# Centring the values and initial states in the projection stage, and a chunk norm whose variance comes spread over channels

## The chip, the cores and the metric

The kernel runs on one core of one Trainium2 chip. The metric is the device time of one execution in microseconds (us). A core has TensorE (PE: matmuls, with its weight loads shown apart as PEld), VectorE (DVE), ScalarE (ACT), GpSimd (POOL) and SyncE (SP), which here only issues transfers. Each engine works through its own list of instructions in order; they wait for each other by semaphores.

## What is computed

One layer of a bidirectional mixer over 1,024 latent tokens and 128 context tokens, D_MODEL 1,024, 16 heads of 64 channels, with an MLP behind it. What matters here, from the reference:

```python
S = S * w_t[:, :, None, :] + sa[..., None] * b_t[:, :, None, :] + v_t[..., None] * k_t[:, :, None, :]
...
wkv = ys[0] + ys[1]
mu = jnp.mean(wkv, axis=-1, keepdims=True)
var = jnp.mean(jnp.square(wkv - mu), axis=-1, keepdims=True)
ln = ((wkv - mu) * lax.rsqrt(var + LNX_EPS)).reshape(B, T, D_RWKV) * p['lnx_w'] + p['lnx_b']
x_a = (ln + (bonuses[0] + bonuses[1]).reshape(B, T, D_RWKV)).astype(xn.dtype) * g_out
```

The scan output `y` of a token is linear in the values `v` and in the initial state along the value channel. If each value vector and each state column has its mean over the 64 value channels taken off beforehand, `y` comes out with mean zero over its head. The bonus still needs the values as they are. Context tokens start from a zero state, and their final states are outputs that need the uncentred values.

## The kernel before

Channels lie on the 128 partitions, two heads (a *pair*) at a time, so there are 8 pairs. Tokens are cut into 9 chunks of 128: 8 of latents, 1 of context. The order of each engine's work is written out by hand in five blocks of the program (sync, gpsimd, tensor, scalar, vector), and all waits are explicit. There are three stages.

**Projection stage** (function bodies of the loops `for p in range(PAIRS)` on each engine). For each pair PE fills PSUM banks in a fixed list, `Fills` (L104): 12 low-rank fills, then for k, r, v, ks, cc, ch, vt, cb, g, za, bon, zb three fills each (thirds of the tokens, `cg`), g having six. Fill n goes to bank (n + 6) mod 8 and waits until fill n - 8 has been emptied (`freed`, L129), so the fill `g1` of the last third waits for the emptying of `cb` of the first third, and `g0` of the last third for `vt` of the last third. `BY_DVE` (L101) names the fills that DVE empties, in that order; ACT empties the others. `vt` is the transposed values; ACT copies it to `vn` (L1616), SP stores it to HBM (L674), and `vn` also serves as room for the small inversions (`substitution`, L2013). DVE's own list in a pair: running sums of log decays, keys, the substitution of the last pair, the key norm (reciprocal over 1,152 columns, L2057), operands, the product `ch` (L2071), the convolution (L2076 to L2083), the product `cb` (L2088), the bonus (L2093).

**Scan stage**: 72 units, u = 9 p + j (pair p, chunk j; j = 8 is the context chunk). In loop step s PE runs turn, token_major, ur_state, the first Gram products of unit s + 4, serial_ur, `spread`, left, y_state, the second Gram products, serial_u, right, `mean`, serial_s, serial_y, `gate` and `variance` (L1348 to L1388). DVE in step s runs `reciprocal`, the addition of half the outputs (`y_add`, L2161: for j = 4 to 7 of the step before), `turned`, `carried`, Gram mask 0, `scaled`, `summed`, `centred`, the new states, Gram mask 1 (L2202 to L2233). The masks (`gram`, L2106) copy the one Gram PSUM tile out; PE may fill it again only then. In steps 9 to 23 DVE also does pieces of the last pair's substitution before and after.

The norm of a finished chunk (`finals`, L177) goes: PE sums y over channels (`mean`), DVE subtracts (`centred`), ACT squares, PE sums the squares per head into 2 columns (`variance`, one row per token), ACT takes the root of 128x2 (`deviation`), DVE the reciprocal of 128x2, PE spreads it back over channels (`spread`), DVE scales. The last five chunks are done together behind the scan (`TAIL`, L187).

**Dense stage**: 77 block products with their own split of weights and activations.

## Time and profile before

| what | value |
|---|---|
| median of 3 runs | 2705.92 us (2702.68 to 2709.07) |
| the profiled execution: its time | 2705.67 us |
| its span in the profile | 2703.6 us |
| PE busy | 2580.1 us, 95% |
| DVE busy | 1852.0 us, 68% |
| ACT busy | 1080.2 us, 40% |
| POOL busy | 1175.8 us, 43% |
| chain that ended last | PE 85%, DVE 7%, issue 2%, DMA 2%, ACT 2% |

The profile is of one execution; its 2705.67 us are 2703.6 us of span and 2.1 us around it. Busy time adds up the instructions of an engine; the chain follows the work that ended last back through its releasers. In rows of the timeline the columns are start, duration of the group, engine, line, operation, out<-in, count, and in brackets the idle time just before and who ended it.

### The profile page before, as it was taken

To read this page: it belongs to the slowest core of one execution; us is meant where nothing else is said; L and a number is where in the kernel's file an instruction comes from. 1 tells how busy PE (TensorE), PEld (TensorE's weight loads), DVE (VectorE), ACT (ScalarE), POOL (GpSimd) and SP (SyncE) were. 2 spreads that over 40 slices of the span, in tenths; PEclk is the share of its full clock that TensorE was granted. 3 is DMA by queue.
4 is the path that set the end of the run, shared out by engine and by line. 5 is a ranking of instruction groups with operands and counts; after the bars stand their busy time and mean duration, and the time that the engine had idled before them with its cause. 6 is when DMAs were issued, how large, how long until landed. Compare 5 with 4: busy or idle time off the path is not lost.

```text
span 2703.6 us, 68164 instructions
## 1 busy us (share of the span) xinstructions
PE 2580.1 (95%) x28864; PEld 2430.1 (90%) x28864; DVE 1852.0 (68%) x3010; ACT 1080.2 (40%) x1978; POOL 1175.8 (43%) x1154
## 2 busy tenths in 40 slices
PE   4899999999999998999999997999799999999998
PEld 3899999999999996788878887999799999999998
DVE  3464665846748464787766666799778679678686
ACT  3434243342433422433333343443453353443534
POOL 1323222322223224555555544656446556565662
PEclk8999999999999999999999999999899999999999
DMA  8333425435254363444454456454223232333231
GB/s 323 106 110 109 144 69 181 125 97 158 62 174 128 94 193 108 131 143 144 138 154 137 139 160 195 131 175 105 63 63 79 81 101 70 79 84 102 65 79 71
DMA packets 282412, 329.15 MB, mean 122 GB/s; under 512 B 76288, under 2 KB 215936, under 8 KB 273536
## 3 DMA queue, kind: packets, MB, share of 16 engines
q1 hardware_dynamic: 274448, 278.66, 33.2%
q0 software_dynamic: 5904, 39.32, 6.9%
q10 hardware_dynamic: 1760, 6.82, 0.6%
q8 instruction: 231, 3.78, 0.6%
q14 instruction: 69, 0.57, 0.1%
HBM read 221.83 MB, written 91.36 MB: 116 GB/s over the span
## 4 chain that ended last, share of the span: by engine, by line
PE 85%; DVE 7%; issue 2%; DMA 2%; ACT 2%; SPq 1%; POOL 0%; DVEq 0%; ACTq 0%; POOLq 0%
PE ser L970 18%; PE gbank L970 13%; PE bank L970 11%; PE inv L970 11%; PE gbank L1411 8%; PE inv L1411 8%; PE ser L1411 7%; PE bank L1411 7%; DVE a_sum L2298 1%; DMA ring<-in_wblocks 1%; PE inv L1172 1%; PE bank L1155 1%; DVE a_sum L2302 1%; DVE a_sum L2306 1%; DVE a_lo L2272 1%
## 5 line engine op out<-in xcount | busy, mean ns | idle before, releaser
L952 POOL TENSOR_TENSOR w_lo<-raw_w,w_hi 128x512 fp32r<-128x512 f32 x264 | 425.3, 1624 | 370.2 <-ACT w_hi L1747 370.1
L847 POOL TENSOR_TENSOR wsp<-ring,wsp 128x1024 fp32r<-128x1024 f32 x67 | 210.8, 3146 | 670.7 <-ACT wsp L1513 670.7
L1747 ACT ACTIVATE w_hi<-raw_w 128x512 fp32r<-128x512 f32 x264 | 165.1, 632 | 262.5 <-PE ser L1411 98.4
L970 PE MATMUL ser<-xn_hi,wsp 128*128 128x384 f32 x816 | 217.7, 340 | 6.1 <-POOL xn_lo L853 6.1
L1411 PE MATMUL gbank<-a_hi,w_hi 128*128 128x288 f32 x616 | 185.7, 302 | 30.6 <-POOL w_lo L952 14.6
L970 PE MATMUL gbank<-xn_hi,wsp 128*128 128x384 f32 x800 | 213.0, 339 | 1.1 <-issue 1.1
L970 PE MATMUL bank<-xn_hi,wsp 128*128 128x384 f32 x800 | 211.1, 338 | 2.2 <-POOL wsp L847 2.2
L970 PE MATMUL inv<-xn_hi,wsp 128*128 128x384 f32 x800 | 211.3, 338 | 0.5 <-issue 0.5
L2108 DVE TENSOR_TENSOR gmat<-gbank,gmask 128x1024 f32<-128x1024 f32 x144 | 175.6, 1219 | 49.8 <-PE gbank L970 49.0
L1733 ACT ACTIVATE a_hi<-a_sum 128x1152 fp32r<-128x1152 f32 x88 | 103.1, 1173 | 224.6 <-DVE a_sum L2306 78.0
L970 PE MATMUL gbank<-ub 64*64 64x128 f32 (+1 forms) x3456 | 178.4, 310 | 9.5 <-DVE gmat L2108 5.6
L1411 PE MATMUL gbank<-a_hi,w_lo 128*128 128x288 f32 x616 | 184.7, 300 | 0.0
L1411 PE MATMUL gbank<-a_lo,w_hi 128*128 128x288 f32 x616 | 184.4, 299 | 0.0
L1411 PE MATMUL inv<-a_hi,w_lo 128*128 128x288 f32 x616 | 183.9, 299 | 0.0
L1411 PE MATMUL inv<-a_hi,w_hi 128*128 128x288 f32 x616 | 183.7, 298 | 0.0
L1411 PE MATMUL inv<-a_lo,w_hi 128*128 128x288 f32 x616 | 183.6, 298 | 0.0
L1411 PE MATMUL ser<-a_hi,w_hi 128*128 128x288 f32 x616 | 181.6, 295 | 1.5 <-ACT r L1786 1.5
L1411 PE MATMUL bank<-a_hi,w_lo 128*128 128x288 f32 x616 | 181.8, 295 | 0.0
L1411 PE MATMUL ser<-a_hi,w_lo 128*128 128x288 f32 x616 | 181.7, 295 | 0.0
L1411 PE MATMUL ser<-a_lo,w_hi 128*128 128x288 f32 x616 | 181.4, 294 | 0.0
L1411 PE MATMUL bank<-a_lo,w_hi 128*128 128x288 f32 x616 | 181.4, 294 | 0.0
L1411 PE MATMUL bank<-a_hi,w_hi 128*128 128x288 f32 x616 | 181.3, 294 | 0.0
(398 smaller groups left out, 7534.7 us busy)
## 6 DMA issues: line engine op xcount, KB each, us to landing
ring<-in_wblocks SPq DMA_DIRECT2D x107, 512.0 KB, 4.8
ub<-op_d SPq DMA_DIRECT2D x144, 256.0 KB, 2.8
raw_w<-in_wquads SPq DMA_DIRECT2D x33, 1024.0 KB, 4.8
raw_w<-in_wquads POOLq DMA_DIRECT2D x22, 1024.0 KB, 8.8
op_d<-ar SPq DMA_DIRECT2D x32, 576.0 KB, 5.4
op_d<-bk SPq DMA_DIRECT2D x32, 576.0 KB, 6.2
raw_w<-in_wquads SPq DMA_DIRECT2D x44, 256.0 KB, 3.3
raw_w<-zsum POOLq DMA_DIRECT2D x11, 1024.0 KB, 12.3
```

The source lines that it names most:

```text
L847: GT(wsp[s % 2][1][:], ring[(N_ADA_RING + s) % RING][:], wsp[s % 2][0][:].bitcast(F32), ALU.subtract).then_inc(S["wsplit_lo"], 1)
L952: GT(w_lo[n % 4][:], src, w_hi[n % 4][:].bitcast(F32), ALU.subtract).then_inc(S["wl_ok"], 1)
L970: return nc.tensor.matmul(out, lhsT, rhs, start=start, stop=stop)
L1155: ins = nc.tensor.transpose(banks[3][:, y * P:(y + 1) * P], ub[v % LOADS][:, y // 2, 2 + y % 2, :], ident[:])
L1172: ins = nc.tensor.transpose(inv[:, 0, x * P:(x + 1) * P], xt[:, place_of(v), :, :].rearrange("p h t -> p (h t)"), ident[:])
L1411: return nc.tensor.matmul(out, lhsT, rhs, start=start, stop=stop, skip_group_check=True)
L1733: A(a_hi[:, places2(q, j), :], src, ACT.Copy).then_inc(S["ah_ok"], 1)
L1747: A(w_hi[s][:], raw_of(op)[:, m, :].rearrange("p (k c) -> p k c", k=KH), ACT.Copy).then_inc(S["wh_ok"], 1)
L2108: V.tensor_tensor(gmat[v % SETS][:, d, :, :, :].rearrange("p h x t -> p h (x t)"), gbank[:, :, :], gmask[:, d:d + 1, :].to_broadcast([P, 2 ...
L2272: V.tensor_tensor(a_lo[:, places2(q, j), :], src, a_hi[:, places2(q, j), :].bitcast(F32), sub).then_inc(S["al_ok"], 1)
L2298: ch.step(V.tensor_tensor(o[j], a11[j], a12[j], sub))
L2302: ch.step(V.tensor_tensor(o[j], o[j], a22[j], add))
```

## The change

It moves the centring to where values and states are made. DVE instead of ACT empties `vt` (`BY_DVE`): per pair three sums over 64 channels (`tensor_reduce`) and three passes that subtract the mean, the context chunk's mean being held at zero. `first_state` centres the initial states with a sum and a scale. In the scan, `mean` and `centred` are left out for latent chunks and stay for the context chunk. `variance` multiplies the squares by the 64x64 block of ones, so that 128x128 come out with each channel holding its head's sum; ACT's root and DVE's reciprocal then run over 128x128 in SBUF (tile `fsq`), the product `spread` goes away, and `scaled` multiplies two SBUF operands.

```diff
-BY_DVE = ("ch", "cb", "bon")
+BY_DVE = ("ch", "vt", "cb", "bon")
...
+        vmean = sb(dense, "vmean", [P, G, 2 * G])
...
-        fstd = sb(sc, "fstd", [P, 5, 2])
+        smean = sb(sc, "smean", [P, 2])
...
             def mean(p, c, n):
-                name, seen = y_seen(NC * p + (max(c, NC_LAT - 1 - c) if c < NC_LAT else NC_LAT))
-                pe.wait_ge(S[name], seen)
+                if c == NC_LAT:
+                    name, seen = y_seen(NC * p + NC_LAT)
+                    pe.wait_ge(S[name], seen)
                 if 0 < n < TAIL[0][2]:
                     pe.wait_ge(S["xa_ok"], n)
+                if c < NC_LAT:
+                    return
...
             def variance(p, c, n):
                 pe.wait_ge(S["ysq_ok"], n + 1)
-                for b in halves_of:
-                    ins = mm(column(n)[b, :], fsq[:, n % 5, b], bones[:, 0:P:HD], True, True)
+                for hs in halves_of:
+                    ins = mm(place(n, 1)[hs, :], bones[hs, hs], fsq[hs, n % 5, :], True, True)
                 ins.then_inc(S["var_full"], 1)
-
-            def spread(p, c, n):
-
-                pe.wait_ge(S["rec_ok"], n + 1)
-                for h in range(2):
-                    ins = mm(place(n, 1)[halves_of[h], :], fstd[:, n % 5, h:h + 1].to_broadcast([P, HD]), ident[:], True, True)
-                ins.then_inc(S["spread_full"], 1)
...
-                if n < TAIL[0][2]:
-                    pe.wait_ge(S["yc_ok"], n + 1)
+                if n < TAIL[0][2] and c == NC_LAT:
+                    pe.wait_ge(S["yc_ok"], p + 1)
...
-                if p:
-                    act.wait_ge(S["so_v"], 16 * p)
-                    act.wait_ge(S["x_out"], 64 * Q * p)
-                empty(p, "vt", lambda cg: vn[:, cols(cg)], ACT.Copy)
...
             def squares_of(p, c, n):
-                act.wait_ge(S["yc_ok"], n + 1)
+                if n >= 5:
+                    act.wait_ge(S["xa_ok"], n - 4)
+                if c < NC_LAT:
+                    name, seen = y_seen(NC * p + max(c, NC_LAT - 1 - c))
+                    act.wait_ge(S[name], seen)
+                else:
+                    act.wait_ge(S["yc_ok"], p + 1)
                 A(fsq[:, n % 5, :], yf[p % 2][:, c * C:(c + 1) * C], ACT.Square).then_inc(S["ysq_ok"], 1)
...
-                A(fstd[:, n % 5, :], column(n), ACT.Sqrt, scale=1.0 / HD, bias=eps_t[:, 1:2]).then_inc(S["std_ok"], 1)
+                A(fsq[:, n % 5, :], place(n, 1), ACT.Sqrt, scale=1.0 / HD, bias=eps_t[:, 1:2]).then_inc(S["std_ok"], 1)
...
+            def value_tokens(p):
+
+                n = [2 * G] * (G - 1) + [2 * G - 2]
+                for cg in range(G):
+                    x = full(p, "vt", cg).rearrange("p (g v) -> p g v", v=HD)
+                    ch.step(V.tensor_reduce(vmean[:, cg, 0:n[cg]], x[:, 0:n[cg], :], mybir.AxisListType.X, add))
+                ch.settle()
+                if p:
+                    dve.wait_ge(S["so_v"], 16 * p)
+                    dve.wait_ge(S["x_out"], 64 * Q * p)
+                for cg in range(G):
+                    x = full(p, "vt", cg).rearrange("p (g v) -> p g v", v=HD)
+                    stt(vn[:, cols(cg)].rearrange("p (g v) -> p g v", v=HD), bc(vmean[:, cg, :], HD), -1.0 / HD, x, mul, add).then_inc(ev["D"], 1)
...
                     V.tensor_tensor(cct[:, cols(cg)], x, cct[:, cols(cg)], mul).then_inc(ev["D"], 1)
+                value_tokens(p)
...
+                s0 = pl[p % 2][:, PL_ST:PL_ST + 2 * HD]
+                ch.step(V.tensor_reduce(smean[:], s0.rearrange("p (d v) -> p d v", v=HD), mybir.AxisListType.X, add))
+                ch.settle()
+                ch.step(V.tensor_scalar(smean[:], smean[:], -1.0 / HD, None, mul))
+                ch.settle()
...
             def centred(p, c, n):
-                dve.wait_ge(S["mu_full"], n + 1)
+                if c < NC_LAT:
+                    return
+                dve.wait_ge(S["mu_full"], p + 1)
...
-                V.reciprocal(fstd[:, n % 5, :], fstd[:, n % 5, :]).then_inc(S["rec_ok"], 1)
+                V.reciprocal(fsq[:, n % 5, :], fsq[:, n % 5, :]).then_inc(S["rec_ok"], 1)
...
-                dve.wait_ge(S["spread_full"], n + 1)
-                ch.step(V.tensor_tensor(y, y, place(n, 1), mul))
+                dve.wait_ge(S["rec_ok"], n + 1)
+                ch.step(V.tensor_tensor(y, y, fsq[:, n % 5, :], mul))
```

How the order of the instructions moves is shown at three places. The first is DVE in the projection stage, from the product `ch` to the product `cb` of one pair. Before:

```order
L2071 TENSOR_TENSOR cct<-gbank,cct 128x384 x2
L2071 TENSOR_TENSOR cct<-bank,cct 128x384
L2076 TENSOR_SCALAR cv<-cct,pk 128x1152
L2079 SCALAR_TENSOR_TENSOR cv<-cct,pk,cv 128x16x63
L2079 SCALAR_TENSOR_TENSOR cv<-cct,pk,cv 128x127
L2082 SCALAR_TENSOR_TENSOR cv<-cct,pk,cv 128x16x63
L2083 SCALAR_TENSOR_TENSOR cv<-cct,pk,cv 128x127
L2088 TENSOR_TENSOR cv<-ser,cv 128x384 x2
L2088 TENSOR_TENSOR cv<-gbank,cv 128x384
```

The same place in the changed kernel:

```order
L2074 TENSOR_TENSOR cct<-gbank,cct 128x384 x2
L2074 TENSOR_TENSOR cct<-bank,cct 128x384
L2036 TENSOR_REDUCE vmean<-bank 128x6
L2036 TENSOR_REDUCE vmean<-inv 128x6
L2036 TENSOR_REDUCE vmean<-inv 128x4
L2043 SCALAR_TENSOR_TENSOR vn<-vmean,bank 128x384
L2043 SCALAR_TENSOR_TENSOR vn<-vmean,inv 128x384 x2
L2080 TENSOR_SCALAR cv<-cct,pk 128x1152
L2083 SCALAR_TENSOR_TENSOR cv<-cct,pk,cv 128x16x63
L2083 SCALAR_TENSOR_TENSOR cv<-cct,pk,cv 128x127
L2086 SCALAR_TENSOR_TENSOR cv<-cct,pk,cv 128x16x63
L2092 TENSOR_TENSOR cv<-ser,cv 128x384 x2
```

Six instructions over three PSUM fills now stand between the product `ch` and the convolution, ahead of the product that empties `cb`.

The second place is DVE in a scan step in which it also adds outputs (`yf<-ser`), from Gram mask 1 to Gram mask 0. Before:

```order
L2180 SCALAR_TENSOR_TENSOR yf<-bank,yf 128x128
L2157 SCALAR_TENSOR_TENSOR state<-ser,gstep,stg 128x64 x2
L2108 TENSOR_TENSOR gmat<-gbank,gmask 128x1024
L2184 RECIPROCAL fstd<-fstd 128x2
L2168 TENSOR_TENSOR yf<-ser,yf 128x2x128
```

and in the changed kernel:

```order
L2166 SCALAR_TENSOR_TENSOR state<-ser,gstep,stg 128x64 x2
L2112 TENSOR_TENSOR gmat<-gbank,gmask 128x1024
L2195 RECIPROCAL fsq<-fsq 128x128
L2177 TENSOR_TENSOR yf<-ser,yf 128x2x128
L2118 TENSOR_TENSOR tc<-inv,trimc 128x384
```

The reciprocal keeps its place ahead of the addition of the outputs and is 64 times as wide; the centring ahead of the states is gone.

The third place is PE in a scan step, from the first part of the second Gram product through the gate and variance. Before, `spread` is the row `ident,fstd` ahead of left, and the mean stands ahead of serial_s:

```order
L970 MATMUL ser<-vb,gmat 64x64 x8
L970 MATMUL bank<-ident,fstd 64x128 x2
L970 MATMUL inv<-xtb,gmat 64x64 x4
L970 MATMUL inv<-xtb,lm 64x64 x8
L970 MATMUL ser<-ub,state 64x128 x4
L970 MATMUL gbank<-ub 64x128 x8
```

and in the changed kernel, from there to the variance:

```order
L971 MATMUL ser<-vb,gmat 64x64 x8
L971 MATMUL inv<-xtb,gmat 64x64 x4
L971 MATMUL inv<-xtb,lm 64x64 x8
L971 MATMUL ser<-ub,state 64x128 x4
L971 MATMUL gbank<-ub 64x128 x8
L971 MATMUL ser<-ur,tt 64x64 x8
L971 MATMUL inv<-p,tc 64x64 x12
L971 MATMUL gbank<-ub 64x256 x4
L971 MATMUL ser<-up,tok 64x64 x2
```

`spread` is gone between serial_ur and left, and no mean stands between the Gram product over 256 columns and serial_s.

## Rows read from the trace of the kernel before

**Rows 1.** Busy time by stage (engine, count), granted clock (PEclk), DMA: projection, scan.

```profile
86.00:1010.00 924.00, 915.01 (x6233) 893.55 (x6234) 544.34 (x916) 354.80 (x544) 248.85 (x82) 1.00 0.40 123
1045.00:1628.00 583.00, 576.06 (x14289) 468.09 (x14283) 403.41 (x970) 223.57 (x606) 295.16 (x642) 1.00 0.48 142
```

**Rows 2.** Timeline of PE in one scan step: gate, variance, turn.

```profile
1269.21 0.39 PE L970 MATMUL bank<-gl,pl 128*64 128x128 f32 x4
1269.42 0.23 PE L970 MATMUL bank<-bones,fsq 128*64 128x2 f32 x4
1269.59 0.55 PE L1172 MATMUL inv<-ident,xt 128*128 128x128 f32 x3
```

**Rows 3.** Timeline of DVE: Gram mask 0 in steps without a chunk norm.

```profile
1050.58 1.22 DVE L2108 TENSOR_TENSOR gmat<-gbank,gmask 128x1024 f32<-128x1024 f32 x1 [0.68 <-PE gbank L970]
...
1058.00 1.22 DVE L2108 TENSOR_TENSOR gmat<-gbank,gmask 128x1024 f32<-128x1024 f32 x1 [0.68 <-PE gbank L970]
```

**Rows 4.** Timeline of DVE: reciprocal and mask 0, steps with a norm, ACT copying y.

```profile
1270.07 0.16 DVE L2184 RECIPROCAL fstd<-fstd 128x2 f32<-128x2 f32 x1
...
1271.90 1.23 DVE L2108 TENSOR_TENSOR gmat<-gbank,gmask 128x1024 f32<-128x1024 f32 x1 [0.64 <-PE gbank L970]
...
1279.85 1.22 DVE L2108 TENSOR_TENSOR gmat<-gbank,gmask 128x1024 f32<-128x1024 f32 x1 [0.63 <-PE gbank L970]
```

**Rows 5.** Groups by line and shape: reciprocals on DVE, the square on ACT.

```profile
L2057 DVE RECIPROCAL kk<-kk 128x1152 f32<-128x1152 f32 x8 | 58.8, 7353 | 0.3
...
L2184 DVE RECIPROCAL fstd<-fstd 128x2 f32<-128x2 f32 x72 | 11.4, 159 | 15.0 <-ACT fstd L1681 14.9
...
L1675 ACT ACTIVATE fsq<-yf 128x128 f32<-128x128 f32 x72 | 21.9, 309 | 5.7 <-DVE yf L2180 4.1
```

**Rows 6.** Timelines of ACT, DVE and PEld in a step where DVE adds outputs.

```profile
1304.47 0.26 ACT L1681 ACTIVATE fstd<-bank,eps_t 128x2 f32<-128x2 f32 x1 [1.06 <-PE bank L970]
...
1304.84 0.16 DVE L2184 RECIPROCAL fstd<-fstd 128x2 f32<-128x2 f32 x1
1304.91 0.41 DVE L2168 TENSOR_TENSOR yf<-ser,yf 128x256 f32<-128x256 f32 x1
...
1305.37 0.32 PEld L970 LDWEIGHTS ser<-state,ub 64*64 64x64 f32 x16 [0.27 <-DVE yf L2168]
...
1306.77 1.23 DVE L2108 TENSOR_TENSOR gmat<-gbank,gmask 128x1024 f32<-128x1024 f32 x1 [0.57 <-PE gbank L970]
```

**Rows 7.** Timeline of DVE: end of the substitution and mask 0, step 19.

```profile
1197.23 0.38 DVE L2036 TENSOR_TENSOR r<-r 72x110 f32<-72x110 f32 x1
1197.65 1.23 DVE L2108 TENSOR_TENSOR gmat<-gbank,gmask 128x1024 f32<-128x1024 f32 x1
```

**Rows 8.** Timeline of DVE: mask 0 in a fifth step (j = 4) and at a pair's turn (j = 0).

```profile
1298.72 1.22 DVE L2108 TENSOR_TENSOR gmat<-gbank,gmask 128x1024 f32<-128x1024 f32 x1 [0.50 <-PE gbank L970]
...
1338.00 1.22 DVE L2108 TENSOR_TENSOR gmat<-gbank,gmask 128x1024 f32<-128x1024 f32 x1 [0.27 <-PE gbank L970]
```

**Rows 9.** Timelines in the fourth pair's projection: DVE products, PE's last g fills.

```profile
530.60 1.01 DVE L2071 TENSOR_TENSOR cct<-inv,cct 128x384 f32<-128x384 f32 x2
...
530.73 0.19 PEld L970 LDWEIGHTS bank<-xn_hi,wsp 128*128 128x128 f32 x1 [0.28 <-DVE cct L2071]
...
535.69 0.56 DVE L2088 TENSOR_TENSOR cv<-gbank,cv 128x384 f32<-128x384 f32 x1
...
536.54 0.88 PE L970 MATMUL gbank<-ar,bk 64*64 64x64 f32 x48
```

**Rows 10.** Timeline behind the scan: five reciprocals, first scaling, first dense products.

```profile
1632.69 0.78 DVE L2184 RECIPROCAL fstd<-fstd 128x2 f32<-128x2 f32 x5 [1.03 <-ACT fstd L1681]
...
1634.33 0.29 DVE L2189 TENSOR_TENSOR yf<-yf,inv 128x128 f32<-128x128 f32 x1 [0.86 <-PE inv L970]
...
1644.45 0.58 PE L1411 MATMUL gbank<-a_hi,w_hi 128*128 128x288 f32 x1 [10.23 <-POOL w_lo L952]
...
1645.78 0.44 PE L1411 MATMUL gbank<-a_hi,w_lo 128*128 128x288 f32 x1
```

**Rows 11.** Groups: one of the dense products on PE.

```profile
L1411 PE MATMUL gbank<-a_hi,w_lo 128*128 128x288 f32 x616 | 184.7, 300 | 0.0
```

More of the change, by code:

```diff
@@ L1303, in mean @@
                 ins.then_inc(S["mu_full"], 1)
-            def column(n):
-                i = n - TAIL[0][2]
-                return banks[2][:, 4 * P - 2:4 * P] if i < 0 else ser[:, 1, 2 * i:2 * i + 2]
             def variance(p, c, n):
                 pe.wait_ge(S["ysq_ok"], n + 1)
-                for b in halves_of:
-                    ins = mm(column(n)[b, :], fsq[:, n % 5, b], bones[:, 0:P:HD], True, True)
+                for hs in halves_of:
+                    ins = mm(place(n, 1)[hs, :], bones[hs, hs], fsq[hs, n % 5, :], True, True)
                 ins.then_inc(S["var_full"], 1)
-            def spread(p, c, n):
-                pe.wait_ge(S["rec_ok"], n + 1)
-                for h in range(2):
-                    ins = mm(place(n, 1)[halves_of[h], :], fstd[:, n % 5, h:h + 1].to_broadcast([P, HD]), ident[:], True, True)
-                ins.then_inc(S["spread_full"], 1)
             def gate(p, c, n):
                 pe.wait_ge(S[f"pl_in{p % 2}"], 16 * (p // 2 + 1))
-                if n < TAIL[0][2]:
-                    pe.wait_ge(S["yc_ok"], n + 1)
+                if n < TAIL[0][2] and c == NC_LAT:
+                    pe.wait_ge(S["yc_ok"], p + 1)
                 for b in halves_of:
@@ L1339, in modulation_turned @@
                 if g:
-                    pe.wait_ge(S["yc_ok"], finals(NC * g + 3)[0][2] + 1)
+                    pe.wait_ge(S["xa_ok"], finals(NC * g + 3)[0][2])
                 for b in range(4):
@@ L1362, in _ @@
                         pe.wait_ge(S["ada_ok"], p + 1)
-                for x in finals(s - 1):
-                    spread(*x)
                 if inverses:
@@ L1388, in _ @@
                     variance(*x)
-            for x in finals(UNITS - 1):
-                spread(*x)
             pe.wait_ge(S["tok_ok"], UNITS)
@@ L1399, in _ @@
                 variance(*x)
-            for x in TAIL:
-                spread(*x)
             pe.wait_ge(S["xa_ok"], UNITS)
@@ L1666, in y_out, with place @@
                     A(y, ser[:, 1, 2 * P:(2 + n) * P].rearrange("p (n t) -> p n t", t=P), ACT.Copy).then_inc(S["ya_ok"], 1)
-            def column(n):
+            def place(n, k):
                 i = n - TAIL[0][2]
-                return banks[2][:, 4 * P - 2:4 * P] if i < 0 else ser[:, 1, 2 * i:2 * i + 2]
+                if i < 0:
+                    return banks[2][:, k * P:(k + 1) * P]
+                return banks[(0, 4, 2)[k] + i // 4][:, (i % 4) * P:(i % 4 + 1) * P]
             def squares_of(p, c, n):
-                act.wait_ge(S["yc_ok"], n + 1)
+                if n >= 5:
[5 more added lines that the diff above has]
+                    act.wait_ge(S["yc_ok"], p + 1)
                 A(fsq[:, n % 5, :], yf[p % 2][:, c * C:(c + 1) * C], ACT.Square).then_inc(S["ysq_ok"], 1)
@@ L2041, in substitution @@
                             done[d] = ch.n
+            def value_tokens(p):
[10 more added lines that the diff above has]
+                    stt(vn[:, cols(cg)].rearrange("p (g v) -> p g v", v=HD), bc(vmean[:, cg, :], HD), -1.0 / HD, x, mul, add).then_inc(ev["D"], 1)
             halves(0)
+            ch.step(V.memset(vmean[:, G - 1, 2 * G - 2:2 * G], 0.0))
             dve.wait_ge(ev["A"], FL.emptied("l", 2)[1])
@@ L2130, in first_state @@
                 dve.wait_ge(S[f"pl_in{p % 2}"], 16 * (p // 2 + 1))
+                s0 = pl[p % 2][:, PL_ST:PL_ST + 2 * HD]
[3 more added lines that the diff above has]
+                ch.settle()
                 for d in range(2):
                     c = chunk(d, 0)
-                    V.tensor_scalar(state[d][0][:], pl[p % 2][:, PL_ST + d * HD:PL_ST + (d + 1) * HD], emid[:, p, d, c:c + 1], None, mul).then_inc(S["s_ok"], 1)
+                    V.tensor_scalar(state[d][0][:], s0[:, d * HD:(d + 1) * HD], smean[:, d:d + 1], emid[:, p, d, c:c + 1], add, mul).then_inc(S["s_ok"], 1)
             def carried(u):
@@ L2236, in _ @@
                 scaled(*x)
-            dve.wait_ge(S["mu_full"], UNITS)
+            dve.wait_ge(S["mu_full"], PAIRS)
             for x in TAIL:
@@ L2242, in _ @@
             dve.wait_ge(S["gate_full"], UNITS)
-            dve.wait_ge(S["spread_full"], UNITS)
             for x in TAIL:
```

4 lines of the change are left out of this document (1 added, 3 removed).

## The prediction

> **What bounds the kernel now.** I read the busy time by stage first. In both stages that the change touches PE is busy nearly throughout, 915.0 of 924 us and 576.1 of 583 us, while DVE is busy for 544 and 403 us [rows 1]. So whatever leaves PE should count, and whatever goes to DVE should be free, as long as no PE instruction waits for it. The averages cannot tell that. I therefore went through the timeline of single scan steps and of one pair's projection, looking at the idle time ahead of the DVE instructions for which PE waits. That idle time is all the room there is.
>
> In the scan one loop matters: PE makes Gram product 0 of unit s + 4, DVE masks it out (mask 0), and only then may PE write the next into the same tile. Mask 0 follows the reciprocal, the addition of outputs, `turned` and `carried` in DVE's list. In a plain step DVE idles 0.64 us before it [rows 4]; where DVE adds outputs 0.57 us [rows 6]; at a pair's turn 0.27 us and in a fifth step 0.50 us [rows 8]; in the fifteen steps with the substitution nothing: 1197.23 + 0.38 ends at 1197.61 and mask 0 starts at 1197.65 [rows 7]. There is a second tie. In 22 steps with mask 0, and in the last four, DVE adds outputs right behind the reciprocal, and PE's next weights wait for exactly that, already for 0.27 us [rows 6].
>
> **What leaves PE in the scan.** Two steps without a norm are 7.42 us apart, two with it 7.95 us [rows 3, 4]: mean, gate, variance and spread show as 0.53 us together. The gate, four records over 128 columns, takes 0.21 us to the next start, the old variance 0.17 us [rows 2]. The mean has the gate's size: 0.21 us saved. Three products of 0.21 and one of 0.17 would be 0.80; the 0.27 that does not show must be where PE waits for another anyway, between the two Gram products, and there stands `spread`. Its removal is worth 0 to 0.21 us; I take 0.03, since mask 0 takes 1.22 us in every step. The wider variance costs 0.04 us.
>
> **What comes to DVE in the scan.** The reciprocal takes 7353 ns over 1,152 columns and 159 ns over 2 [rows 5], so 6.26 ns a column; 126 more columns are **0.79 us**. It also starts later. The variance now takes the gate's 0.39 us instead of 0.23 until its last result [rows 2], 0.16 later. ACT's root over 128 columns costs what the square does, 0.31 us instead of 0.26, 0.05 later [rows 5, 6]. The root used to end at 1304.73, 0.11 before the reciprocal began [rows 6]. So it starts 0.10 later and what is behind it comes **0.89 us** later. That `centred` goes (about 0.3 us) helps nobody: it stood ahead of the states, which wait for PE. `scaled` over two SBUF operands stands behind mask 0, where DVE has time; I take nothing for it.
>
> The Trainium skill (VectorE: DVE Perf Modes, First, the fixed hardware budget) says the reciprocal is an iterative divide with a repeat count of 8. As an estimate from that page and its 0.96 GHz that is 8.3 ns a column, a further 0.26 us in each step and some 17 us on the total. The trace does not agree, it has 6.26 [rows 5], and the sum goes by the trace.
>
> **Steps, one kind at a time** (the reciprocal runs in 66 loop steps):
> - DVE adds outputs, no substitution, 22 steps before the last four: PE waits 0.89 longer, less 0.21 and 0.03: +0.65 each, 14.3 us.
> - Substitution, 15 steps: no idle time, 0.89 - 0.21 = +0.68, 10.2 us. Two of them are turns and two are fifth steps, +1.5 us for all four.
> - Turn of a pair, 5 steps: the centring of the first state comes on top. No row has a sum over channels; its bounds are 0 and the 0.56 us of a product over 384 columns [rows 9]; for its 128 columns and the small scale, each with a wait, I take 0.48. Behind a mask that ends late the root is no longer the limit: 0.48 + 0.79 - 0.27 - 0.21 = +0.79, 4.0 us.
> - Plain, 15 steps: 0.89 - 0.64 - 0.21 = +0.04, 0.6 us.
> - Fifth step, 5: the reciprocal waits for ACT, so 0.16 + 0.05 + 0.79 = 1.00, less 0.50; the mean of the context chunk stays: +0.50, 2.5 us.
> - The last four have no Gram product ahead, so spread's 0.21 counts: 1.00 - 0.42 = +0.58, 2.3 us.
>
> The scan comes to **+35 us**. Behind it stand five norms at once. Before, 1.64 us lay between the first reciprocal and the first scaling [rows 10]; now five reciprocals at 0.87 from start to start are 4.35, and the first begins some 0.3 later: **+3 us**. The dense stage's first product waits for the last scaling, so all of it counts.
>
> **The projection.** ACT loses three copies a pair, which cost nothing before and save nothing. DVE gets three sums and three subtractions over 384 columns of PSUM. Two products of that shape take 1.01 us and one 0.56 [rows 9], so 0.46 each in a row; six are 2.8, and with the wait between them 2.9 us. Bounds are 2.3 us (a sum half as dear) and 3.8 us (each pass at its 0.56 and more for the broadcast operand). DVE's idle time later in the pair does not cover them, because of where they stand: ahead of the convolution and of the product that empties `cb`. PE's last g fills wait for `cb`'s first third. It was emptied at 536.25, and PE started those fills at 536.54 [rows 9]: 0.29 us of room. PE also waits for DVE at this place already, 0.28 us at the product `ch` [rows 9], so the two are in step. PE stalls 2.9 - 0.29 = **2.6 us in each of 8 pairs, 21 us**. What is late next is nothing: the bonus of each pair has over 13 us of idle DVE before it. SP's store of `vn` and its next weight load come about 11 us later, and the ring of four blocks at 12.7 us each covers that.
>
> The sum: 35 + 3 + 21 = 59 us. Against the profiled execution's own 2705.67 us that is **2765 us**; the median of the runs, 2705.92, is the same within 0.3 us. About 0.2% is what a measurement of this kernel can tell from no change.
>
> **Rivals.**
> - *The projection hides it.* If the passes cost little or PE can fill something else, only scan and tail remain: 2706 + 38 = 2744. For it speaks DVE's 41% of idle time; against it the 0.29 us. Chance 0.11.
> - *The stalls halve PE's clock.* After PE's 10.23 us wait the dense products took 0.44 us where they average 0.30 [rows 10, 11], so the granted clock was at 1.2 of 2.4 GHz for a while. If each projection stall does that for some 4 us, 2 us are lost each time: 59 + 16, 2781 us. The waits here are a quarter as long. Chance 0.08. The Trainium skill (TensorE: Matmul & The Clock Gate, What's actually happening) says that the gate closes when the engine has been idle; for stalls this short no row here shows it.
> - *The additions catch up.* If PE's wait for DVE's addition does not carry over and only mask 0 holds, 22 steps cost 0.89 - 0.57 - 0.21 = 0.11 instead of 0.65, 12 us less: 2753. Chance 0.10.
> - *Faster.* The wide reciprocal costs hardly more than the narrow one. Then 62 means (0.21) less the variance (0.04) are 10.5 us, spread adds up to 2, and if the projection hides its passes as well the time is 2694. It decides the sign of a plain step at 0.64 us of extra DVE work. Rows 5 have 0.79. Chance 0.04, as both must hold.
> - *It does not do what it says.* If the centring costs in one place what it saves in the other, about 2706. Chance 0.02.
>
> My forecast has 0.65. The range reaches from 2743, which holds the first and third rival, to 2788, with the dearer passes (3.8 us: +7), a scan 5 to 8 us dearer if `scaled` is held up by POOL, and the clock. Faster by over 0.2%: 0.04; within: 0.02; slower: 0.94.
>
> **What would show it.** In the new profile the reciprocal should last 0.94 us, PE should wait for `yf` of DVE for about 1.1 us in steps with an addition, the idle time before mask 0 should be gone in plain steps, and steps should be 8.0 us (plain) and 8.7 us (addition) apart. PE should stand 2.6 us before the last g fills of each pair. If reciprocals last under 0.4 us or the g fills do not wait, I am wrong.

## The result: 106 us slower, where 59 were forecast

| | before | after |
|---|---|---|
| median | 2706.19 us (2702.68 to 2709.07, 4 runs) | 2812.0 us (2810.03 to 2817.16, 4 runs) |
| span of the profiled execution | 2703.6 us | 2808.0 us |
| first mask 0 of the scan starts | 1018.44 us | 1076.17 us |
| from there to the first dense product | 626.0 us | 674.8 us |
| from the first dense product to the end | 1059.2 us | 1057.1 us |

The ratio is 1.0395, with a 95% interval of 1.0375 to 1.0414. The sign was right; the time of 2812 us is 24 us above the range, which ended at 2788. The projection lost 58 us where 21 were forecast, scan and tail 49 where 38 were; the dense stage gave 2 back. The stages of the changed kernel by busy time, to be held against [rows 1] (the last three columns are the granted clock as a share of full speed, the DMA share and GB/s):

```profile
86.00:1068.00 982.00, 925.67 (x6234) 903.72 (x6235) 613.02 (x966) 346.71 (x520) 258.90 (x82) 0.97 0.38 116
1103.00:1728.00 625.00, 582.74 (x13703) 444.87 (x13701) 440.85 (x923) 229.82 (x604) 296.04 (x642) 1.00 0.45 133
```

In the projection PE idles 56 us, it was 9. It is also *busy* 11 us longer with the same instructions, and the granted clock is 0.97 instead of 1.00. What ended the idle time of PE ahead of the products of its helper (line 971; before, 970), over the whole program, with times:

```profile
its engine sat idle before it (us, times) until:
  DVE cv L2092: 52.9, 8
  DVE yf L2177: 27.1, 32
  DVE gmat L2112: 16.2, 27
```

Before, `gmat` stood in this list with 5.6 us, the addition `yf` with 1.6 us, and `cv` was not in it. The wait for `cv` is at the place that the prediction named, PE's last g fills. Here is the fourth pair on DVE, then POOL, then PE, with [rows 9] as their counterpart (`...` marks rows left out, here and below):

```profile
555.31 1.01 DVE L2074 TENSOR_TENSOR cct<-inv,cct 128x384 f32<-128x384 f32 x2
556.24 1.01 DVE L2036 TENSOR_REDUCE vmean<-ser 128x6 f32<-128x384 f32 x2
557.16 0.41 DVE L2036 TENSOR_REDUCE vmean<-gbank 128x4 f32<-128x256 f32 x1
557.61 1.02 DVE L2043 SCALAR_TENSOR_TENSOR vn<-vmean,ser 128x384 f32<-128x384 f32 x2
558.55 0.55 DVE L2043 SCALAR_TENSOR_TENSOR vn<-vmean,gbank 128x384 f32<-128x384 f32 x1
559.01 0.81 DVE L2080 TENSOR_SCALAR cv<-cct,pk 128x1152 f32<-128x1152 f32 x1
559.86 1.53 DVE L2083 SCALAR_TENSOR_TENSOR cv<-cct,pk,cv 128x1008 f32<-128x1008 f32 x2
561.43 3.24 DVE L2086 SCALAR_TENSOR_TENSOR cv<-cct,pk,cv 128x1008 f32<-128x1008 f32 x1
564.59 2.69 DVE L2087 SCALAR_TENSOR_TENSOR cv<-cct,pk,cv 128x127 f32<-128x127 f32 x1
567.37 0.56 DVE L2092 TENSOR_TENSOR cv<-gbank,cv 128x384 f32<-128x384 f32 x1
...
561.18 2.42 POOL L848 TENSOR_TENSOR wsp<-ring,wsp 128x1024 fp32r<-128x1024 f32 x1 [10.32 <-ACT wsp L1499]
563.57 3.57 POOL L860 TENSOR_TENSOR kd_r<-kd,kd_r 128x1152 fp32r<-128x1152 f32 x1
...
568.08 1.56 PE L971 MATMUL gbank<-ar,bk 64*64 64x64 f32 x48 [6.57 <-DVE cv L2092]
```

The six passes last from 556.24 to 559.01, 2.77 us, as forecast (2.8 to 2.9). But two instructions of the convolution that the change does not touch have grown: the one over 1,008 columns from 1.27 to 3.24 us, the one over 127 columns from 0.35 to 2.69, together by 4.3 us in each of the 8 pairs. The delay of 2.77, the growth of 4.31 and the room of 0.29 give 2.77 + 4.31 - 0.29 = 6.8; PE stands 6.57. The 3.24 us end at 564.67, 1.07 behind the end of POOL's weight split at 563.60; the 2.69 end at 567.28, 0.14 behind the end of POOL's split of `kd` at 567.14, which itself takes 3.57 us and not 2.67. This looks as if the later convolution had run into POOL; the experiments below test it. In the kernel before it ended at 535.25 + 0.34 = 535.59, and POOL began 0.8 us behind it, as POOL's timeline of the same pair there shows:

```profile
536.40 2.39 POOL L847 TENSOR_TENSOR wsp<-ring,wsp 128x1024 fp32r<-128x1024 f32 x1 [10.25 <-ACT wsp L1513]
538.74 2.67 POOL L859 TENSOR_TENSOR kd_r<-kd,kd_r 128x1152 fp32r<-128x1152 f32 x1
```

The clock around this stall on PE (columns: stretch, length, busy time with instructions, granted clock, DMA share, GB/s):

```profile
560.00:568.00 8.00, 1.51 (x96) 0.81 0.45 141
568.00:571.00 3.00, 2.92 (x52) 0.50 0.48 167
571.00:572.00 1.00, 1.00 (x5) 0.58 0.86 241
572.00:576.00 4.00, 4.00 (x25) 1.00 1.02 381
```

PE works again from 568.08, and until about 571.8 at 1.2 of 2.4 GHz: half of 3.7 us is lost in this pair. Over the 8 pairs PE is busy 10.7 us longer (925.67 against 915.01). That is less than eight times this loss: by the granted clock over the ten us behind each stall, 0.79 to 0.83, 15.0 us are lost, and the rows don't say where some 4 were made good. So the loss of 58 us is 52.9 of stalls and 10.7 of longer busy time, less some 6 us of other short waits that are gone.

In the scan, a step with an addition, on ACT, DVE and PE (before: [rows 6]):

```profile
1381.84 0.37 ACT L1669 ACTIVATE fsq<-bank,eps_t 128x128 f32<-128x128 f32 x1 [1.36 <-PE bank L971]
...
1382.24 0.95 DVE L2195 RECIPROCAL fsq<-fsq 128x128 f32<-128x128 f32 x1 [0.25 <-ACT fsq L1669]
1383.11 0.36 DVE L2177 TENSOR_TENSOR yf<-ser,yf 128x256 f32<-128x256 f32 x1
...
1384.92 1.23 DVE L2112 TENSOR_TENSOR gmat<-gbank,gmask 128x1024 f32<-128x1024 f32 x1 [0.49 <-PE gbank L971]
...
1383.52 0.46 PE L971 MATMUL ser<-state,ub 64*64 64x64 f32 x16 [0.82 <-DVE yf L2177]
```

The reciprocal takes 0.95 us and PE waits 0.82 us for the addition (about 1.1 were forecast), with mask 0 still having 0.49 us of idle time ahead of it. This is the forecast mechanism. What is larger: DVE now waits 0.25 us for the root ahead of the reciprocal. And on PE, gate, variance and turn follow each other differently (before: [rows 2]):

```profile
1272.58 0.39 PE L971 MATMUL bank<-gl,pl 128*64 128x128 f32 x4
1272.90 0.44 PE L971 MATMUL bank<-fsq,bones 64*64 64x128 f32 x4
1273.27 0.55 PE L1173 MATMUL inv<-ident,xt 128*128 128x128 f32 x3
```

From gate to variance are 0.32 us where 0.21 were, from variance to turn 0.37 where 0.17 were: the variance costs PE 0.31 us more, not the forecast 0.04.

### The profile page after: what moved, and what is told of

It is laid out like the page before. It is cut to its first block, busy times and chain, and to the rows that moved or that the text cites. A ratio compares the mean times of both kernels' runs of the same rounds, so it can differ in the third digit from the quotient of the medians.

```text
span 2808.0 us, 66936 instructions
## 1 busy us (share of the span) xinstructions
PE 2598.5 (93%) x28320; PEld 2418.0 (86%) x28320; DVE 1962.5 (70%) x3011; ACT 1080.5 (38%) x1954; POOL 1188.1 (42%) x1154
## 4 chain that ended last, share of the span: by engine, by line
PE 48%; DVE 9%; issue 3%; ACT 2%; SPq 0%; DMA 0%; POOL 0%; DVEq 0%; ACTq 0%; POOLq 0%
PE ser L971 9%; PE gbank L1397 8%; PE inv L1397 7%; PE ser L1397 7%; PE bank L1397 7%; PE gbank L971 4%; PE inv L971 3%; PE bank L971 2%; DVE a_sum L2308 1%; DVE gmat L2112 1%; DVE a_sum L2312 1%; DVE a_sum L2316 1%; DVE fsq L2195 1%; DVE a_lo L2282 1%; ACT fsq L1669 1%
```

## The experiments

Twelve kernels ran, in four groups; each group has its own runs of the kernel before, and every comparison is by the ratio to those. As measure of a step I take the distance between the starts of two masks 0 in rows of DVE's timeline: from j = 1 to 2 (plain), from j = 5 to 6 (addition), from j = 8 to the next pair's j = 0 (turn), and from j = 1 to 2 of the second pair (substitution). The value is the one on which most pairs agree within 0.02 us; single steps of every execution are up to some 2 us longer, at other places each time (in the changed kernel PE stood 1.41 us in one of them and waited for nothing that the profile shows), and are left out. Rows with a plus are the kernel "centred behind cb" with one more edit, "the last" is the row above, and a dash stands where the steps are not read.

| kernel | ratio to before (95%) | plain | addition | turn | substitution |
|---|---|---|---|---|---|
| before | 1 | 7.95 | 8.05 | 7.83 | 7.94 |
| the change | 1.0395 (1.0375 to 1.0414) | 8.08 | 8.89 | 8.77 | 9.01 |
| values copied by ACT | 1.0187 (1.0168 to 1.0207) | 8.07 | 8.89 | 8.75 | 9.01 |
| kd split waits | 1.0349 (1.0334 to 1.0365) | - | - | - | - |
| both splits wait | 1.0261 (1.0245 to 1.0278) | - | - | - | - |
| centred behind cb | 1.0167 (1.0147 to 1.0187) | 8.07 | 8.89 | 8.75 | 9.00 |
| + addition first | 1.0062 (1.0041 to 1.0082) | 8.07 | 8.07 | 8.75 | 9.00 |
| + variance over 128 rows | 1.0111 (1.0087 to 1.0134) | 7.85 | 8.74 | 8.75 | 8.50 |
| + reciprocal of 2 columns | 1.0005 (0.9996 to 1.0014) | 8.00 | 8.16 | 8.14 | 8.00 |
| + reciprocal behind mask 0 | 1.0009 (0.9998 to 1.0019) | 8.00 | 8.00 | 8.14 | 7.99 |
| the last, variance over 128 rows | 0.9970 (0.9960 to 0.9980) | 7.85 | 7.85 | 8.14 | 7.90 |
| narrow variance, no mean | 0.9932 (0.9920 to 0.9944) | 7.72 | 7.83 | 8.13 | 7.72 |
| the last, addition first | 0.9925 (0.9913 to 0.9937) | 7.73 | 7.76 | 8.14 | 7.72 |
| before, values centred behind cb | 0.9967 (0.9955 to 0.9980) | - | - | - | - |

### The projection: two theories for the stall

My theory was that POOL holds up the convolution; the rival, that the two instructions are slow by themselves, for instance through the store of `vn` that starts at the same time.

**Values copied by ACT** (the values stay uncentred):

```diff
-BY_DVE = ("ch", "vt", "cb", "bon")
+BY_DVE = ("ch", "cb", "bon")
...
+                empty(p, "vt", lambda cg: vn[:, cols(cg)], ACT.Copy)
...
-                value_tokens(p)
```

> The changed kernel with ACT copying the transposed values as before; their centring is left out (the initial states' stays), the scan is the changed one. From the profile of the changed kernel PE stands 52.9 us in front of the last g fills, and the first mask 0 of the scan comes 57.7 us later than before. Theory A (that is all the projection's loss, and it is all due to the three sums and three subtractions): about 2812 - 58 = 2754 us. Rival B (part of the 57.7 us has another cause, such as the scan's prologue or the larger context): over 2765. What is left over 2706 is then the price of the scan and its tail, 48 us, against the 38 that were forecast.

2760.16 us against 2710.3; first mask 0 at 1022.2 us. The ratio falls by 0.0208, which is 56 us where 58 were expected: theory A. Scan and tail alone cost 50 us.

**POOL's split of kd waits for the convolution**, the passes staying where they are:

```diff
                 if p >= 0 and STREAM[b] == "cb":
+                    pool.wait_ge(S["conv_ok"], p + 1)
                     plane_low(kd_r[0], kd[0], kd_r[1], 4 * p + 3)
```

> The changed kernel, but POOL waits for the end of DVE's convolution before it starts the split of kd (kd_r). Theory A (DVE's last convolution instruction over 127 columns takes 2.69 us instead of 0.35 because POOL's split runs on SBUF at the same time): it falls back to about 0.35 us, PE's stall in front of the last g fills goes from 6.57 to about 4.2 us, and the time by 8 times 2.3, to about 2793 us; the 1008-column one before it stays at 3.24 us, since POOL's split of weights still meets it. Rival B (the instruction is slow for a reason of its own, such as the store of vn that runs at the same time): 2.69 us stays, 2812 us. Rival C (POOL's later split makes PE wait for kd_r in the bonus): DVE as in A, but the time over 2800.

DVE's and POOL's timelines in the fourth pair:

```profile
556.23 3.23 DVE L2087 SCALAR_TENSOR_TENSOR cv<-cct,pk,cv 128x1008 f32<-128x1008 f32 x1
559.38 0.34 DVE L2088 SCALAR_TENSOR_TENSOR cv<-cct,pk,cv 128x127 f32<-128x127 f32 x1
...
555.90 2.49 POOL L848 TENSOR_TENSOR wsp<-ring,wsp 128x1024 fp32r<-128x1024 f32 x1 [10.24 <-ACT wsp L1500]
559.80 2.63 POOL L860 TENSOR_TENSOR kd_r<-kd,kd_r 128x1152 fp32r<-128x1152 f32 x1 [1.41 <-DVE cv L2088]
```

The 127 columns are back at 0.34 us, POOL's split at 2.63, and PE's stall fell from 6.57 to 4.29 us: theory A for this instruction. The time fell only by 0.0046, 12 us, not by 18. That is the time of rival C, but not its mechanism: in the projection PE has no wait for `kd_r`. What the trace shows is that PE is busy 933.6 us in the projection, 8 more than in the changed kernel. In part that is the clock. In the fourth pair it was at half from 565.0 to 571.8 us in the changed kernel, and PE stood through 3 of these 6.8 us; here it is at half from 558.5 to 565.3, and PE stands through 2. Over the ten us behind each stall 18.3 us are lost by the granted clock where 15.0 were, which is 3.3 of the 8; the rest is open.

**Both splits wait:**

```diff
                 p, b = divmod(s - 2 - N_LORA, PAIR_BLOCKS)
+                if p >= 0 and STREAM[b] == "cb":
+                    pool.wait_ge(S["conv_ok"], p + 1)
+                split_low(s)
```

> As the run before, but POOL also waits for the convolution before the weight split that comes ahead of it. Theory A: both convolution instructions are back at 1.27 and 0.35 us, PE's stall in front of the last g fills falls to 6.57 - 4.3 = 2.3 us, the 2.6 that were forecast, and the time to about 2812 - 34 = 2778 us, or up to 10 us more if PE then waits for the weights that POOL splits later. Rival B (POOL has no part in it): the two instructions stay at 3.24 and 2.69 us, 2812 us or above.

DVE, POOL and PE, fourth pair:

```profile
549.50 1.27 DVE L2088 SCALAR_TENSOR_TENSOR cv<-cct,pk,cv 128x1008 f32<-128x1008 f32 x1
550.68 0.35 DVE L2089 SCALAR_TENSOR_TENSOR cv<-cct,pk,cv 128x127 f32<-128x127 f32 x1
551.12 0.56 DVE L2094 TENSOR_TENSOR cv<-gbank,cv 128x384 f32<-128x384 f32 x1
...
551.11 2.38 POOL L848 TENSOR_TENSOR wsp<-ring,wsp 128x1024 fp32r<-128x1024 f32 x1 [12.18 <-DVE cv L2089]
...
551.83 0.93 PE L973 MATMUL gbank<-ar,bk 64*64 64x64 f32 x48 [2.25 <-DVE cv L2094]
```

2782.26 us, the ratio down by 0.0134, 36 us where 34 were expected. With POOL out of the way the convolution is at its old 1.27 and 0.35 us and the stall is 2.25 us, against 2.6 in the forecast. The rival has fallen. The clock, though, dropped behind seven of the eight stalls, which last 2.24 to 2.33 us, for the fourth pair like this:

```profile
552.00:553.00 1.00, 1.00 (x50) 1.00 0.06 20
553.00:557.00 4.00, 4.00 (x16) 0.57 0.89 261
557.00:561.00 4.00, 4.00 (x25) 1.00 0.97 371
```

Behind the fifth stall, of 2.30 us, it stayed at full, and PE got 78 instructions into six us instead of 68:

```profile
667.64:673.64 6.00, 6.00 (x78) 1.00 0.73 208
```

**Centred behind cb.** ACT copies as before; DVE sums and subtracts in `vn` when it would idle, and SP stores `vn` behind `cv`:

```diff
+                filled(p, "vt")
+                ch.step(V.tensor_reduce(m[:, 0:k], x[:, 0:k, :], mybir.AxisListType.X, add))
+                ch.settle()
+                stt(x[:, 0:k, :], bc(m[:, 0:k], HD), -1.0 / HD, x[:, 0:k, :], mul, add).then_inc(S["conv_ok"], 1)
...
                         sp.dma_start(xb_d[p], cv[:]).then_inc(S["xb_out"], 16)
+                        sp.wait_ge(S["conv_ok"], 2 * p + 2)
+                        sp.dma_start(v_d[p].rearrange("c t v -> t c v"), a3(vn[:])).then_inc(S["so_v"], 16)
```

> The changed kernel with another place for the centring of values: ACT copies the transposed values to vn as before, and DVE sums and subtracts in vn behind the product that empties cb, in the 13 us in which it was idle; SP stores vn behind the store of cv. The computation is whole. Theory A (only the place ahead of the convolution costs): as the run with ACT's copy alone, about 2754 us, no PE stall in front of the g fills. Rival B (two passes over 1024 columns in SBUF meet POOL there, or the later store holds up SP's weight loads): 5 to 20 us more than that run, with a new wait of PE for ring or for the bonus.

2755.06 us, where about 2754 were expected; the two passes take 1.21 and 1.56 us, and no wait for `cv` is left on PE. Theory A. The kernels below are built on this one.

### The scan: what holds a step

**Reciprocal behind mask 0**, the same length, another place:

```diff
-                for x in finals(s - 1):
-                    reciprocal(*x)
+                if j == 4:
+                  for x in finals(s - 1):
+                      reciprocal(*x)
...
                     gram(s + 4, 0)
+                for x in finals(s - 1) * (j != 4):
+                    reciprocal(*x)
```

> The run with values centred behind cb, and in the scan DVE's wide reciprocal moved from its place ahead of the addition, turned, carried and mask 0 to behind mask 0 (except in the fifth steps). The computation is whole. Theory A (the reciprocal costs by what is queued behind it on DVE, not by its length): addition steps fall from 8.89 to about 7.85 us, plain ones from 8.07 to about 7.75, below the 8.05 and 7.95 of before, since the mean product is gone; the fifteen substitution steps keep about half of their loss (9.0 to 8.5), since DVE has no idle time there; the tail keeps its 3 to 4 us. Time 2755 - 38 = about 2717 us, 2708 if the substitution steps lose nothing. Rival B (DVE is simply loaded by 0.79 us more a step): steps stay within 0.2 us of the last run, 2745 to 2755. Rival C (scaled comes so late that the additions to xt behind it hold up PE's turn): a new wait of PE for xt, 2725 to 2745.

2706.32 us against 2704.63. The ratio fell by 0.0158, 43 us, where 38 were expected (47 with the substitution steps whole; the one of the second pair is, at 7.99). Plain and addition steps are both at 8.00 us; mask 0 has idle time ahead of it again:

```profile
1304.74 0.41 DVE L2174 TENSOR_TENSOR yf<-ser,yf 128x256 f32<-128x256 f32 x1
1305.14 0.56 DVE L2115 TENSOR_TENSOR tc<-inv,trimc 128x384 f32<-128x384 f32 x1
1305.62 0.48 DVE L2148 TENSOR_SCALAR stg<-state,gstep 128x64 f32<-128x64 f32 x2
1306.87 1.23 DVE L2109 TENSOR_TENSOR gmat<-gbank,gmask 128x1024 f32<-128x1024 f32 x1 [0.77 <-PE gbank L970]
```

So a wide reciprocal costs nothing where nothing urgent is queued behind it, in the substitution steps either. But two numbers don't fit my theory: plain steps should have come to 7.75 and addition steps to 7.85.

**Reciprocal of 2 columns** at its old place (126 of 128 are left out):

```diff
-                V.reciprocal(fsq[:, n % 5, :], fsq[:, n % 5, :]).then_inc(S["rec_ok"], 1)
+                V.reciprocal(fsq[:, n % 5, 0:2], fsq[:, n % 5, 0:2]).then_inc(S["rec_ok"], 1)
```

> The run with values centred behind cb, but DVE's reciprocal takes 2 of the 128 columns; the inversion of the other 126 is left out. Theory A: the reciprocal starts 0.33 us later against the gate than before (variance 0.10, root 0.23) and was 0.79 us longer; without the 0.79 the addition steps fall from 8.89 to 8.1 us, the plain ones from 8.07 to 7.8, the substitution steps from 9.0 to 8.2, and the tail gives 3 to 4 us back. Over 66 steps that is 22 x 0.79 + 15 x 0.27 + 15 x 0.79 + 5 x 0.79 + 4 x 0.79 + 4, about 45 us: 2710 us. Rival B (the later start and the scaling over two SBUF operands are what costs): no more than 20 us of the 45 come back, over 2735.

2706.64 us: the ratio fell by 0.0162, 44 of the 45 us. Theory A for the reciprocal, and again 8.00 us in plain steps, now with 0.77 us of idle time ahead of mask 0. PE holds them at 8.00, DVE doesn't.

**Addition first**, the wide reciprocal between it and `turned`:

```diff
+                if there(s - 1):
+                    y_add(s - 1)
                 for x in finals(s - 1):
                     reciprocal(*x)
...
-                if there(s - 1):
-                    y_add(s - 1)
```

> The run with values centred behind cb and the wide reciprocal at its place ahead of turned, carried and mask 0, but DVE adds the outputs ahead of it. Theory A (two ties, each with its own steps: the addition holds 26 steps, mask 0 the others): addition steps fall from 8.89 us to about 8.2, now held by mask 0 or by PE's 8.0, while plain steps stay at 8.07 and substitution steps at 9.0: 2755 - 22 x 0.7 = about 2740 us. Rival B (the addition is not what PE waits for; turned or mask 0 is, and the trace names the last of several): addition steps stay over 8.7 us, 2752 or more.

2721.48 us, better than expected. Addition steps fall by 0.82 us to just the 8.07 of plain ones, which don't move: two ties with their own steps, as forecast. The ratio fell by 0.0105, 28 us. Other steps with an addition fell by more than the one in the table: the next one by 1.08 (8.89 to 7.81, below the plain steps), the one behind it by 0.89. In the profiled executions the time from the first mask 0 to the last is 20.8 us shorter, and from there to the first dense product, where the last four steps have an addition too, 5.0 us. So the scan accounts for 25.8 of the 28.

**Variance over 128 rows.** `bones` is block-diagonal, so contracting all rows gives the same sums, in the shape of the gate:

```diff
                 for hs in halves_of:
-                    ins = mm(place(n, 1)[hs, :], bones[hs, hs], fsq[hs, n % 5, :], True, True)
+                    ins = mm(place(n, 1)[hs, :], bones[:, hs], fsq[:, n % 5, :], True, True)
```

> The run with the reciprocal behind mask 0, and the wide variance contracted over all 128 rows: each half takes 128x64 of the block-diagonal ones and all rows of the squares, the shape of the gate ahead of it, instead of 64x64 and 64 rows. The result is the same. In the last runs gate and wide variance took 0.32 and 0.37 us to the next start, where gate and narrow variance took 0.22 and 0.17, and steps bound by PE stood at 8.00 us with it and at 7.73 without. Theory A (the change of shape on PE, 128 rows to 64 and back to 128, costs the 0.3 us): gate 0.22 and variance about 0.21, steps bound by PE at 7.75, 66 x 0.26 = 17 us less than the run with the reciprocal behind mask 0, about 2690. Rival B (the variance costs by its 128 columns alone): steps stay at 8.00 us, 2706. Rival C (the wait for ACT's squares holds it): 0.32 stays ahead of the variance, only the 0.37 falls, 2698.

> The run with values centred behind cb, its reciprocal at its place, and only the shape of the variance changed, to 128 rows. Theory A (in addition steps a loop runs variance, root, reciprocal, addition, PE's step, variance, so what PE gains ahead of the root counts there too): addition steps from 8.89 to about 8.7 us, plain ones, held by mask 0, from 8.07 to 7.9, 2755 - 12 = about 2743. Rival B (DVE holds the steps whatever the variance costs on PE): within 4 us of the run it is compared with.

PE's timeline of the first of the two:

```profile
1293.01 0.39 PE L970 MATMUL bank<-gl,pl 128*64 128x128 f32 x4
1293.22 0.39 PE L970 MATMUL bank<-fsq,bones 128*64 128x128 f32 x4
1293.54 0.55 PE L1172 MATMUL inv<-ident,xt 128*128 128x128 f32 x3
```

Gate 0.21, variance 0.32, together 0.53 us: 0.16 less than with 64 rows, and 0.15 less in each step bound by PE (8.00 to 7.85). That is half of what I expected from the change of shape; the other 0.15 over the narrow variance stays, so theory A and rival B each hold half. Rival C has the time (2698) but not the rows: it is the 0.32 ahead of the variance that fell. 2697.63 us, 0.0039 or 10.5 us less than with the reciprocal behind mask 0, and 66 x 0.15 is 9.9. With the reciprocal at its old place the same edit gives 0.0056, 15 us, 0.15 in addition steps and 0.22 in plain ones: the variance stands ahead of the root and so in DVE's loop too. Substitution steps fell by 0.50 there (9.00 to 8.50), three times what PE gains, and no run shows why. The Trainium skill (TensorEngine Tiling (Array Packing), Key Properties) says that changing the tiling mode drains the engine. By that rule the 64-row product between two shapes of 128 rows costs extra. The 0.16 us agree in sign; the page gives no size.

**Narrow variance, no mean**: the kernel before with the centring behind `cb` and of the initial states, its variance and `spread` untouched, `mean` and `centred` left out for latents:

```diff
 def mean(p, c, n):
...
+                if c < NC_LAT:
+                    return
...
 def centred(p, c, n):
-                dve.wait_ge(S["mu_full"], n + 1)
+                if c < NC_LAT:
+                    return
+                dve.wait_ge(S["mu_full"], p + 1)
```

> The kernel before with the centring of values in SBUF behind cb and of the initial states, and without mean and centred for latent chunks; variance, root, reciprocal over 128x2 and spread are as before. The computation is whole. Theory A (leaving out the mean alone is worth its 0.21 us in 62 steps, and the centring costs nothing there): about 13 us under the kernel before, less 5 x 0.3 at the turns of pairs: 2698 against 2710. Rival B (the mean product was hidden between waits for DVE's addition and the masks): within 4 us of the kernel before. Rival C (the passes in SBUF cost in the projection): slower than before.

**Addition first** in this kernel:

```diff
+                if there(s - 1):
+                    y_add(s - 1)
                 for x in finals(s - 1):
                     reciprocal(*x)
```

> As the run with the narrow variance and no mean, and DVE adds the outputs ahead of the reciprocal instead of behind it. Theory A (PE waits for the addition in 26 steps, and it stood behind a reciprocal that waits for ACT's root): another 22 x 0.1 to 0.2 us, so 2 to 4 us less than that run. Rival B (mask 1 holds the start of the addition, not the reciprocal): no difference beyond 1 us. Rival C: spread comes later behind the delayed reciprocal and costs more than the addition gives, 1 to 5 us slower.

2688.61 and 2686.18 us against 2704.63; 2698 against 2710 was expected for the first, so it gained 16 to 18 us where 12 were expected. PE's timeline of the second, with the old shapes:

```profile
1276.27 0.39 PE L971 MATMUL bank<-gl,pl 128*64 128x128 f32 x4
1276.49 0.23 PE L971 MATMUL bank<-bones,fsq 128*64 128x2 f32 x4
1276.65 0.55 PE L1173 MATMUL inv<-ident,xt 128*128 128x128 f32 x3
```

Plain steps are at 7.73 us: without the mean a step saves 0.22 us, as forecast (0.21), and with the product `spread` in it still stands 0.27 below the 8.00 of the wide variance without `spread`. A turn takes 8.13 where it took 7.83; with the mean's 0.22 gone, centring the first state costs 0.52 us. The addition's place is worth 0.07 us a step; the two runs' intervals overlap. The gain of 18 us is more than 62 x 0.22 less 5 x 0.5. So a last run had the scan as before and the values centred behind `cb` alone:

```diff
                     V.tensor_tensor(cv[:, cols(cg)], x, cv[:, cols(cg)], mul).then_inc(ev["D"], 1)
+                value_tokens(p)
```

> The kernel before with one edit: the values are centred in SBUF behind cb and stored behind cv. The scan is as before: it forms and subtracts the mean, which is now zero for latents but for the initial state's part. It prices that placement alone. In the run with the narrow variance and no mean, the first mask 0 of the scan came at 1009.7 us against 1018.4 before, and the whole gained 18 us where 62 x 0.22 less 5 x 0.5 for the turns is 11. Theory A (the later store of vn changes nothing for PE, the 8 us of the projection are the scatter between executions): within 3 us of the kernel before. Rival B (SP's weight loads are no longer behind a store in that place, and PE's short waits for weights go): 5 to 9 us faster. Rival C (passes in SBUF that meet POOL's split of kd, 3.67 us instead of 2.67, cost something in the bonus): 3 to 10 us slower.

2701.15 us against 2709.22, 8 to 9 us faster, the size of rival B. PE's idle time up to 1010 us is 4.6 us instead of 9.0 and the first dense product comes 4.7 us earlier in the profiled execution; a wait of 2.2 us for a weight split and short waits are gone. Whether the later store is the cause wasn't tried.

## Why the prediction was wrong

**What held.** PE was bound where the prediction said, by mask 0 in plain and substitution steps and by the addition in the others (8.08 and 8.89 us, forecast 8.0 and 8.7); the reciprocal took 0.95 us (forecast 0.945); the passes took 2.77 us (2.8 to 2.9); with POOL kept away the stall is 2.25 us (2.6). "Additions catch up" is out: PE waits 0.82 us with mask 0 idle. "The projection hides it" and "faster" are out.

**Step that failed first: the projection, 21 us forecast, 58 measured.** The term "2.9 - 0.29 = 2.6 us in each of 8 pairs" moved the convolution by 2.9 us and kept its length. The forecast asked what stands behind the moved instructions and not what else runs at the time to which they move. POOL's rows for that stretch were there to be read: a weight split of 2.4 us from 536.40 and the split of `kd` from 538.74, the first 0.8 us behind the end of the convolution at 535.6. Moved by 2.8 us, its last two instructions met both. That is 4.3 us in each pair, 34 us over all; with POOL held back they are gone and the time is 36 us shorter, which leaves the kernel at 1.0261. The Trainium skill (SBUF — State Buffer, Who interferes with whom) states that a DVE instruction with two SBUF inputs contends with a GpSimd instruction that reads SBUF, that the port pair which they share is an exclusive lock, and that the order of issue decides who blocks. The traces agree. The convolution reads `cct` and `cv`, both in SBUF, and each of its two instructions ends 0.2 us less than its own length behind POOL's end (1.07 for 1.27, 0.14 for 0.34); POOL's split of `kd`, which began while the first ran, is itself 0.9 us longer. DVE's product that reads one operand from PSUM kept its length beside POOL: 0.56 us from 551.12, with POOL's weight split from 551.11, in the run where both splits wait.

**Second: the clock, a rival at 0.08.** It said 2 us lost for each stall, 16 in all; PE's busy time grew by 10.7 (15.0 by the granted clock), and it came on top of the likeliest case and not in place of it. The reason against it was that "the waits here are a quarter as long", and that no row showed such stalls. The waits were 6.6 us; and at the forecast length the clock fell too, behind seven of eight stalls of 2.24 to 2.33 us. The trace of the kernel before holds two waits of PE that bear on this and that the prediction does not use. These are the five us behind a wait of 3.81 us, and behind one of 2.19 us,

```profile
87.95:92.95 5.00, 5.00 (x20) 0.66 0.80 222
...
877.23:882.23 5.00, 5.00 (x29) 1.00 0.98 343
```

the first at half clock for most of the time, the second at full. So stalls between 2.2 and 2.3 us went either way, and what decides is open.

**Third: the variance, +0.04 us forecast, +0.31 measured.** I costed it by the gate, whose shape it does not have; the nearer row was `mean`, 64 x 64 like it. It counts twice. PE-bound steps stand at 8.00 instead of 7.73. And in DVE's loop the root starts 0.80 us behind the gate's start, where it was 0.50 (forecast +0.16), and takes 0.37 instead of 0.26 (forecast +0.05), so that the reciprocal starts 0.33 later and not 0.10. Over a pair the nine steps were to lose 4.0 us and lost 4.8, and the kinds differ more than the sum: 3.56 in the four with an addition (2.60 forecast), 0.94 at the turn (0.79), 0.12 in each of three plain ones (0.04), and nothing in the fifth step (-0.07, where 0.50 were forecast). A substitution step lost 1.07 instead of 0.68, and from the last mask 0 to the first dense product the loss is 10.1 us, where last four steps and tail were put at 5.

**Right at their size:** the mean (0.22 for 0.21), `spread` worth next to nothing (by the rows 7.73 + 0.31 - 8.00 = 0.04 us, forecast 0.03; no run leaves it out alone), the centring of a first state (0.52 for 0.48).

## What to carry to other kernels

An instruction that is moved later costs its delay and also what it then meets: before summing, lay the other engines' rows beside its new time, here POOL's, since both read SBUF. On an engine with slack ask what is urgent behind a new long instruction: the wide reciprocal cost 44 us ahead of an addition and a mask, and nothing behind them. Cost a small matmul by a row of its own shape between the same neighbours, and try the least part of a change alone: leaving out the mean with values centred in idle time gave 0.9932 of the time before, the whole change 1.0395.

## What the hardware did that was not expected

- A DVE instruction over 127 columns took 2.69 us instead of 0.35 while POOL's subtraction ran over SBUF, and POOL's took 3.57 instead of 2.67; kept apart, both were at their old length in all 8 pairs.
- Stalls of PE of 2.24 to 2.33 us were followed by some 3.4 us at 1.2 of 2.4 GHz in seven cases of eight; the eighth, of 2.30 us, and one of 2.19 us in the kernel before were not.
- The slow stretch can begin while PE still stands (at 565.0 in a stall from 561.5 to 568.1), and a longer stall then covers more of it: 3 of 6.8 us at 6.57 us of standing, 2 of 6.8 at 4.29.
- A product that contracts 128 rows, half of them zeros, was faster on PE than the same sums over 64 rows (gate and variance 0.53 us instead of 0.69), with neighbours of 128 rows.
